# Hybrid conv/attention decoder layer on one core: the first norm's x blocks in halves, the last norm's third product on GpSimd

## The reference

```python
def reference(x, attn_norm_g, w_in, conv_w, ..., final_norm_g):
    h = rmsnorm(x, attn_norm_g)                    # x is 512 x 1024
    proj = h @ w_in                                # u_b, u_c, u_x, q, k, v, g_conv, g_attn
    y_conv = (u_b * short_conv(u_c * u_x, conv_w)) @ w_conv_out
    attn = sliding_window_attention(q, k, v, attn_sinks, rel_bias)
    mixed = sigmoid(g_conv) * y_conv + sigmoid(g_attn) * (attn @ w_attn_out)
    x = x + mixed @ w_o
    h2 = rmsnorm(x, mlp_norm_g)
    x = x + square(relu(h2 @ w_up)) @ w_down
    return rmsnorm(x, final_norm_g)

def rmsnorm(x, g):
    return x * rsqrt(mean(x * x, axis=-1) + 1e-6) * g
```

## Time and profile before

| what | us |
|---|---|
| median of 3 runs | 748.97 |
| lowest, highest | 748.92, 749.09 |
| the profiled execution's own time | 749.23 |
| its span in the profile | 747.5 |
| PE busy | 740.1 (99% of the span) |
| DVE busy | 658.7 (88%) |
| ACT busy | 429.3 (57%) |
| POOL busy | 86.0 (12%) |

### The profile page before, as it was taken

The page is one execution under the profiler, slowest core; times in us unless marked ns, Lnnn a source line. Parts: engine busy times, 40 slices in busy tenths (PEclk is TensorE's granted clock), DMA queues, the critical chain, the costliest instruction groups (busy, mean ns, idle before and its releaser), DMA issues.

```text
span 747.5 us, 10674 instructions
## 1 busy us (share of the span) xinstructions
PE 740.1 (99%) x4194; PEld 649.9 (87%) x4194; DVE 658.7 (88%) x766; ACT 429.3 (57%) x555; POOL 86.0 (12%) x119
## 2 busy tenths in 40 slices
PE   8999999999999999999999999999999999999997
PEld 8898888888888888888888899889988999899985
DVE  6997788989899687989999999998699879986998
ACT  6773555553644557564658776654465455545556
POOL 1610000111122101010100101010101010100102
PEclk9999999999999999999999999999999999999999
DMA  9898223161247987778767847777677768676703
GB/s 325 240 299 275 76 65 105 57 168 58 84 133 238 307 226 200 191 225 200 250 169 178 215 121 214 175 196 198 170 188 199 179 171 216 173 202 181 208 1 114
DMA packets 68948, 134.41 MB, mean 180 GB/s; under 512 B 2653, under 2 KB 18085, under 8 KB 68901
## 3 DMA queue, kind: packets, MB, share of 16 engines
q1 hardware_dynamic: 48880, 85.23, 33.9%
q0 software_dynamic: 19808, 48.25, 30.0%
q10 hardware_dynamic: 212, 0.28, 0.1%
HBM read 127.43 MB, written 6.32 MB: 179 GB/s over the span
## 4 chain that ended last, share of the span: by engine, by line
PE 98%; DMA 1%; ACT 0%; DVE 0%; SPq 0%; issue 0%; ACTq 0%
PE pair L1094 46%; PE pair L1049 22%; PE pair L790 6%; PE pair L792 6%; PE pair L791 6%; PE pair L916 5%; PE pair L837 2%; PE pair L812 1%; PE pair L811 1%; PE pair L821 1%; DMA xn<-in_x 1%; PE pair L851 1%; PE pair L943 0%; PE pair L945 0%; PE pair L944 0%; PE pair L1000 0%
## 5 line engine op out<-in xcount | busy, mean ns | idle before, releaser
L1406 ACT ACTIVATE high<-home_raw 128x2048 fp32r<-128x2048 f32 x91 | 174.3, 1916 | 148.1 <-PE pair L1094 102.4
L2058 DVE TENSOR_TENSOR home_lo<-home_raw,high 128x2048 fp32r<-128x2048 f32 x91 | 208.5, 2291 | 34.4 <-ACT high L1406 34.1
L1094 PE MATMUL pair<-high,s_hi_tile 128*128 128x512 f32 x440 | 110.4, 391 | 0.0
L1094 PE MATMUL pair<-high,s_lo_tile 128*128 128x512 f32 x440 | 109.9, 390 | 0.0
L1094 PE MATMUL pair<-home_lo,s_hi_tile 128*128 128x512 f32 x440 | 109.7, 390 | 0.0
L1094 PEld LDWEIGHTS pair<-home_lo,s_hi_tile 128*128 128x128 f32 x440 | 82.4, 188 | 17.5 <-DVE home_lo L2058 0.4
L1094 PEld LDWEIGHTS pair<-high,s_lo_tile 128*128 128x128 f32 x440 | 82.4, 188 | 17.1
L1094 PEld LDWEIGHTS pair<-high,s_hi_tile 128*128 128x128 f32 x440 | 81.7, 188 | 17.4 <-ACT pair L1501 0.5
L790 PE MATMUL pair<-h,wgt 128*128 128x512 f32 x192 | 76.7, 399 | 0.0
L792 PE MATMUL pair<-h,wgt 128*128 128x512 f32 x192 | 75.0, 391 | 0.0
L791 PE MATMUL pair<-h,wgt 128*128 128x512 f32 x192 | 74.9, 390 | 0.0
(11 more groups left out here) (236 smaller groups left out, 1130.1 us busy)
## 6 DMA issues: line engine op xcount, KB each, us to landing
home_raw<-in_w_up SPq DMA_DIRECT2D x16, 1024.0 KB, 5.3
home_raw<-in_w_down SPq DMA_DIRECT2D x16, 1024.0 KB, 5.1
raw<-in_w_in SPq DMA_DIRECT2D x26, 512.0 KB, 4.9
home_raw<-in_w_up POOLq DMA_DIRECT2D x12, 1024.0 KB, 8.3
home_raw<-in_w_down POOLq DMA_DIRECT2D x12, 1024.0 KB, 8.5
home_raw<-in_w_in POOLq DMA_DIRECT2D x7, 1024.0 KB, 8.6
home_raw<-in_w_in SPq DMA_DIRECT2D x7, 1024.0 KB, 6.2
home_raw<-in_w_conv_out SPq DMA_DIRECT2D x4, 1024.0 KB, 5.2
```

The lines of the kernel that those rows point to most:

```text
L1094: last = mm(pair[region(s, i)][:, b, :], a_[:, k, b * P:(b + 1) * P], w[:, k, :], start=(fresh and kind == 0 and k == 0), stop=(kind == 2 ...
L1406: a(high[n % 2][:, :], home_raw[home_of(s, name)][:, :], ACT.Copy).then_inc(m_hi, 1)
L2058: v.tensor_tensor(home_lo[home][:, :], home_raw[home][:, :], f32(high[n % 2][:, :]), ALU.subtract).then_inc(m_lo, 1)
```

## The change

Seven edits at the start and four at the end:

- x0 and x1 are each loaded as two transfers of 512 columns (x_in for the first half, x_rest for the second). DVE's share of squares waits for the second half, ACT's squares of block 0 for the first half alone, of block 1 for both.
- Block 0 is scaled in two halves, and DVE's order becomes: share of block 0, first half of block 0, share of block 1, second half of block 0, both halves of block 1.
- PE transposes all of block 0 before block 1.
- The low parts of M1's q weights are made in three pieces (rows 0 and 1, row 2, row 3) in place of two, and PE's third pass of M1 waits for each.
- `scale_x(3)` is split around the last `tile_low`, its first half one tile sooner.
- The late transposes wait tile by tile, and block 3's first four come ahead of block 2's last two.
- POOL waits for 6 low pieces in place of 5 before N4's addition (the same point in the order).
- The gain of block 3's early half moves from DVE to POOL, behind those of blocks 0 and 1.
- The root factor of block 1's early half moves from ACT to DVE, behind `scale_late(1)`.
- `scale_late(3)` and its store are cut into two pieces of 256 columns.
- The stores keep their order and are one more.

```diff
-XN_PARTS = ((0, D), (0, D // 2, D), (0, D), (0, D // 2, D))
+XN_PARTS = ((0, D // 2, D), (0, D // 2, D), (0, D), (0, D // 2, D))
...
+        LOW_ROWS = {M1: ((0, 1), (2,), (3,)), N2: ((0, 1), (2, 3))}
...
             def load_x(b):
-                sp.dma_start(xn[:, b, :], x[b * P:(b + 1) * P, :]).then_inc(x_in[b], 16)
+                if b > 1:
+                    sp.dma_start(xn[:, b, :], x[b * P:(b + 1) * P, :]).then_inc(x_in[b], 16)
+                    return
+                for c, done in ((slice(0, D // 2), x_in), (slice(D // 2, D), x_rest)):
+                    sp.dma_start(xn[:, b, c], x[b * P:(b + 1) * P, c]).then_inc(done[b], 16)
...
-            for b, late in ((0, 1), (0, 0), (1, 1), (1, 0), (2, 1), (2, 0), (3, 1)):
...
+            for b in range(TB):
+                for e in range(512 // late_size(b)):
+                    sp.wait_ge(out_late, b + e + 1)
+                    store(b, 512 * (1 - early(b)) + late_size(b) * e, late_size(b))
+                if b < TB - 1:
                     sp.wait_ge(out_early[b], 1)
-                    store(sp, b, early(b))
+                    store(b, 512 * early(b), 512)
...
-            pool.wait_ge(q_low, 5)
+            pool.wait_ge(q_low, 6)
...
             gain(0)
             gain(1)
+            gain(3)
...
-            for b, n in ((0, 1), (1, 0), (0, 2), (1, 1), (0, 3), (1, 2), (1, 3)):
+            for b, n in ((0, 1), (0, 2), (0, 3), (1, 0), (1, 1), (1, 2), (1, 3)):
                 x_pair(b, n)
...
-                        order = [(k, f) for e in range(2) for f in range(4) for k in (2 * e, 2 * e + 1)]
+                        order = [(k, f) for rows in LOW_ROWS[i] for f in range(4) for k in rows]
...
-                            elif k % 2 == 0:
-                                pe.wait_ge(q_low, 2 * at_ + k // 2 + 1)
+                            elif any(k == rows[0] for rows in LOW_ROWS[i]):
+                                pe.wait_ge(q_low, 3 * at_ + [rows[0] for rows in LOW_ROWS[i]].index(k) + 1)
...
             def late_transposes():
-                pe.wait_ge(h_ready, 8)
-                x_transposes(2)
-                x_transposes(3)
+                for b, n in ((2, 0), (2, 1), (2, 2), (3, 0), (3, 1), (2, 3), (3, 2), (3, 3)):
+                    if b == 2:
+                        pe.wait_ge(h_ready, 2 * n + 2)
+                    x_pair(b, n)
...
                 n = SQUARED[b]
+                if b == 1:
+                    act.wait_ge(x_rest[b], 16)
...
             def scale_early(b):
-                if b < 2:
-                    act.wait_ge(gained, b + 1)
-                else:
-                    act.wait_ge(gained_late, 1)
+                act.wait_ge(gained, 3 if b == 3 else b + 1)
...
             root_of(2)
-            scale_early(1)
             root_of(3)
...
-                dve.wait_ge(x_in[b], 16)
+                dve.wait_ge(x_rest[b] if b < 2 else x_in[b], 16)
...
             share_of_squares(0)
+            scale_x(0, (0,))
             share_of_squares(1)
-            scale_x(0)
-            scale_x(1)
+            scale_x(0, (1,))
+            scale_x(1, (0, 1))
...
-            q_low_half(M1, 0)
-            q_low_half(M1, 1)
-            scale_x(2)
+            for e in range(3):
+                q_low_rows(M1, e)
+            scale_x(2, (0,))
             share_of_squares(3)
-            for k in range(4, 8):
+            for k in range(4, 7):
                 tile_low(0, k)
-            scale_x(3)
-            q_low_half(N2, 0)
-            q_low_half(N2, 1)
+            scale_x(3, (0,))
+            tile_low(0, 7)
+            scale_x(3, (1,))
+            for e in range(2):
+                q_low_rows(N2, e)
...
-            def gain(b):
...
+            def scale_early_1():
+
+                dve.wait_ge(gained, 2)
+                r = res[:, 1, 512 * early(1):512 * early(1) + 512]
+                v.tensor_scalar(r, r, rms3[:, 2, 1:2], None, ALU.mult).then_inc(out_early[1], 1)
...
-                v.scalar_tensor_tensor(out=r, in0=src, scalar=rms3[:, 2, b:b + 1], in1=gfin[:, 512 * ch:512 * ch + 512],
-                                       op0=ALU.mult, op1=ALU.mult).then_inc(out_late, 1)
+                acc, n = pair[region(STAGES - 1, N4)][:, 1, :], late_size(b)
+                for c0 in range(0, 512, n):
+                    r = res[:, b, 512 * ch + c0:512 * ch + c0 + n]
+                    v.scalar_tensor_tensor(out=r, in0=acc[:, c0:c0 + n] if b == 3 else r, scalar=rms3[:, 2, b:b + 1],
+                                           in1=gfin[:, 512 * ch + c0:512 * ch + c0 + n], op0=ALU.mult, op1=ALU.mult
+                                           ).then_inc(out_late, 1)
...
             factor(1)
-            gain(3)
             scale_late(1)
+            scale_early_1()
             factor(2)
```

More of the change, by code:

```diff
@@ L354, in build @@
         x_in = [sem(f"x_in{b}") for b in range(TB)]
+        x_rest = [sem(f"x_rest{b}") for b in range(2)]
         raw_in = [sem(f"raw_in{i}") for i in range(4)]
@@ L403, in build @@
         ss3_ready, fin_step = sem("ss3_ready"), sem("fin_step")
-        gained, gained_late = sem("gained"), sem("gained_late")
+        gained = sem("gained")
         out_early, out_late = [sem(f"out_early{b}") for b in range(TB)], sem("out_late")
@@ L515, in early, with late_size @@
             return 0 if b < 2 else 1
+        def late_size(b):
+            return 256 if b == TB - 1 else 512
         block = ctx.enter_context(nc.Block())
@@ L645, in _, with store @@
             sp.dma_start(gfin[:, :], bass.AP(final_norm_g.tensor, 0, [[0, P], [1, D]])).then_inc(gfin_in, 16)
-            def store(eng, b, ch):
-                eng.dma_start(out[rows_of(b), 512 * ch:512 * ch + 512],
-                              res[:, b, 512 * ch:512 * ch + 512]).then_inc(out_done, 16)
-            for b, late in ((0, 1), (0, 0), (1, 1), (1, 0), (2, 1), (2, 0), (3, 1)):
-                if late:
-                    sp.wait_ge(out_late, b + 1)
-                    store(sp, b, 1 - early(b))
-                else:
+            def store(b, c0, n):
+                sp.dma_start(out[rows_of(b), c0:c0 + n], res[:, b, c0:c0 + n]).then_inc(out_done, 16)
+            for b in range(TB):
[3 more added lines that the diff above has]
+                if b < TB - 1:
                     sp.wait_ge(out_early[b], 1)
-                    store(sp, b, early(b))
-            sp.wait_ge(out_done, 16 * 2 * TB)
+                    store(b, 512 * early(b), 512)
+            sp.wait_ge(out_done, 16 * (2 * TB + 1))
         @block.gpsimd
@@ L854, in x_pair @@
                     last.then_inc(xt_ready, 1)
-            def x_transposes(b):
-                for n in range(4):
-                    x_pair(b, n)
             def idle_transposes(n):
@@ L896, in q_product @@
                         elif kind == 2:
-                            pe.wait_ge(q_low, at_ + 3)
+                            pe.wait_ge(q_low, at_ + 4)
                         if i in HS:
@@ L1783, in share_of_squares, with scale_x, q_low_rows @@
                                        ).then_inc(share_done, 1)
[L1785 to L1797, removed]
+            def scale_x(b, parts):
+                if 0 in parts:
+                    dve.wait_ge(root_done, b + 1)
+                    v.reciprocal(rms[:, 1, b:b + 1], rms[:, 0, b:b + 1]).then_inc(rms_step, 1)
+                    dve.wait_ge(rms_step, b + 1)
+                for e in parts:
+                    c = slice(*XN_PARTS[b][e:e + 2])
+                    v.tensor_scalar(xn[:, b, c], xn[:, b, c], rms[:, 1, b:b + 1], None, ALU.mult).then_inc(xn_ready, 1)
+            def q_low_rows(i, e):
+                at_, rows = Q_ORDER.index(i), LOW_ROWS[i][e]
+                c = cols(512 * rows[0], 512 * len(rows))
+                dve.wait_ge(q_high, 4 * at_ + rows[-1] + 1)
                 v.tensor_tensor(q_lo[i][:, c], q_raw[i][:, c], f32(q_hi[at_ % 2][:, c]), ALU.subtract).then_inc(q_low, 1)
```

6 lines of the change are left out of this document (removed).

## The result

| us | before | changed |
|---|---|---|
| median of 6 runs | 749.06 | 752.72 |
| lowest, highest | 748.92, 749.25 | 751.94, 753.01 |
| profiled execution: own time, span | 749.23, 747.5 | 751.94, 750.2 |

The changed kernel is slower: a ratio of 1.0046, interval [1.0036, 1.0056], where 748.25 was forecast and 748.85 was the upper end. Its profiled execution is the fastest of its six, so the trace shows 2.7 us of a difference of 3.66.

A forecast was written before the change was run, and what follows sets the result against it. PE's own work bounds the middle, a backlog of stores the end. Profiled 749.23 - 0.3 (start) - 0.45 (end) = 748.48, or 748.22 beside the median 748.97, given as 748.25; range 747.7 to 748.85.

The forecast's parts named there:

- POOL's third product "is free": End: block 3's gain on POOL takes 2.65 us and has some 5 us of slack before it is wanted.
- "isn't slowed beside it": End: DVE's 2048-column subtraction keeps its time beside POOL, on rows of 2.28 with POOL busy and 2.29 without.
- Rival (d): End: POOL's product lengthens the subtraction at 735.85, delaying PE; 750.55 if they take turns, slower from 0.72 growth; chance 0.04.
- "All else shifts as a block": Middle: only PE's first real work and what follows its last matmul can change the time.
- "I take nothing": Start: no cost for later issue of q rows, x2 and x3 (0.86 us), since the 16 DMA engines are full.
- Rival (e): Start: the whole load is late past 0.86 + 0.3 and the end's gain is spent: 749.0 to 749.3; chance 0.04.
- the second rival: Start: named for the case that the four x pieces come later than the two, by the skill's 1 MiB rule.
- (a): Start: the x halves come late and eat the 0.3: 748.5; chance 0.2.
- The start's -0.3: Start: with block 0 scaled and transposed first, the first matmul comes at about 9.0 in place of 9.31.
- The end's -0.45: End: two stores issued 0.4 to 0.45 sooner fill the bandwidth dip and shrink the store backlog; bounds 0 to -0.8.
- rival (b): End: the tail gives nothing, as nine stores with two short ones need what the dip gave: 748.65; chance 0.12.
- The signs named beforehand: Wrong if block 1's squares start after 6.3, subtraction over 2.35, PE waits between 9 and 740, or stores full to 746.5.

The follow-up runs named there:

- e8: Kernel before with all the end's edits, POOL's gains held by waits until the subtractions are done: 749.51 against 749.19, ratio 1.0003.
- e4: Kernel before with one edit, block 3's gain moved from DVE to POOL: 750.11 against 749.32, ratio 1.0009.
- e9: Kernel before with one more ACT wait at the start, on a load long landed: 750.47 against 749.23, ratio 1.0017.
- e14: Kernel before with the start's edits, but block 0 alone split and no further ACT wait: 751.0 against 749.26, ratio 1.0032.
- e13: Kernel before with x0 and x1 loaded by four transfers of 64 tokens by 1024 columns (4 KB rows): 753.49 against 749.26, ratio 1.005.
- e5: Kernel before with the start's new order but x0 and x1 loaded whole: 749.67 against 749.19, ratio 1.0005.
- e16: Kernel before with two more ACT waits at the start, on a load long landed: 750.49 against 749.22, ratio 1.0015.
- e10: Kernel before with gain(3) behind scale_late(1) on DVE, two lines swapped: 748.95 against 749.23, ratio 0.9995.
- e3: Kernel before with only the end's edits: 750.13 against 749.32, ratio 1.0012.
- e15: Kernel before with gain(3) behind scale_late(1) on DVE, and the last scaling and its store cut in two: 749.06 against 749.26, ratio 1.0.
- e2: Kernel before with only the start's edits: 751.75 against 749.32, ratio 1.003.
- e12: Kernel before with the start's edits, POOL's first two gains held until M3's subtraction is done: 751.21 against 749.23, ratio 1.0026.
- e6: Kernel before with only the loads of x0 and x1 cut in four, old order kept: 752.56 against 749.19, ratio 1.0046.
- e7: Kernel before with POOL's first product also waiting for block 1's early squares: 749.22 against 749.19, ratio 1.0.
- e17: Changed kernel with one further ACT wait at the start, behind the one it adds: 752.74 against 749.22 of the kernel before, ratio 1.0046.

## Why the prediction was wrong, point by point

**POOL's third product "is free", and DVE "isn't slowed beside it": wrong.** I compared 2.28 beside POOL with 2.29 without it and took the equality as proof. The equality was real, but it was a case where POOL waited: two products in 5.29 that take 2.59 alone (e8). Rival (d) named the place, the slack of 0.05 and the price per 0.1, and even that the two might take turns; its chance of 0.04 was far too low and its size (another 2.29) too high. The growth is 1.10, because what the subtraction waits for is one product of POOL, 1.3 alone (e8), and not its own length again. The Trainium skill, GPSIMD Engine Reference, Specifications, states that POOL and DVE contend for shared SBUF interfaces when the DVE instruction has two SBUF inputs. The runs bear it out, 2.29 to 3.39 (e4). I set the page aside for a row that couldn't test it.

**The first meeting wasn't in the forecast at all.** I had the middle as untouched and so "All else shifts as a block". e9 shows that it doesn't: one dead wait on ACT at the start costs 1.24 at the end, since POOL's lead over a subtraction falls from 0.56 to 0.41.

**"I take nothing" for four transfers: wrong in size and in its ground.** The ground was that the engines are full (share 1.03), so that transfers wait for engines and not for SP. With more transfers they weren't full: 0.83 and 0.86. I put block 1 0.1 late, 0.4 if short rows cost, 0.86 if the cover failed; the profiled execution has 0.57, and the others with four half-row pieces 1.08 to 1.82. That spread may be what the median of the changed kernel has beyond its trace, 3.66 against 2.7, but only one of its executions was traced. Rival (e) had the mechanism, at 749.0 to 749.3; the size was again too small. The Trainium skill, DMA: Bandwidth & Descriptors, Rules for kernel authors, wants transfers of 1 MiB or more for full bandwidth; e14 and e13 agree with its direction. (The prediction gave that page to "the second rival"; late loads are rivals (a) and (e).)

**The start's -0.3: not there.** Without the split loads (e5) the first q matmul comes 0.06 sooner. The step that failed is "block 0's eight transposes and the parameter tile are through by about 7.9, block 1's eight run 8.03 to 8.98": with block 0 there, the first pair and the parameter tile alone took PE from 6.80 to 7.50, where three at 0.12 would be 0.36, and then fourteen followed without a gap, 7.50 to 9.25 on PE. DVE's first gain waited for one of them (8.71 where 8.47 was forecast) and the first q matmul waited for DVE's gains. What PE lacked was neither block. e16 says the same: with block 1 read 0.43 sooner, q came at 33.83, within the spread of 33.68 to 33.90.

**The end's -0.45: half there, and given back.** DVE freed early does fill the dip, but the time from ACT's last squares to the end of the span falls by 0.2 to 0.25 (5.33 to 5.13 in e10, 5.08 in e3), not 0.45. In the changed kernel it is 5.42. There the scaling of block 0's late half starts 0.62 behind its reciprocal (741.24 to 741.86), where e10 and e15 have 0.27. Runs with the start's new order but not the end's edits show the same 0.62 and a tail of 5.61 to 5.65 (e2, e5, e12, e14), so the new order comes with 0.3 at the tail and the end's edits give 0.2 back. Why isn't known: e13, in the old order, has it too (0.62, 5.64), and e6 has not (0.27, 5.26). With e5's subtractions and q unchanged, this 0.3 is what its 0.48 has to show in the trace. Of rival (b) one part holds: the short pieces give nothing (e15 beside e10).

**The signs named beforehand** told it rightly: block 1's squares after 6.3 (6.55), a subtraction beside the third product over 2.35 (3.40), PE waiting between 9 and 740 (1.03 for M3's low part).

**The sum.** Medians: the start's edits cost 2.43 (e2), the third product 0.79 (e4), together 3.22 of 3.66. Inside the start the first meeting is worth up to 1.24 (e9) and the rest is the late load and the 0.3 at the tail; e12, with the gains held, still costs 1.98, of which holding POOL takes some (PE waits 0.47 there and 0.38 in e8). How the remaining 0.4 divides isn't settled, since block 1's landing differs by over 1 us from run to run.

## What to carry to other kernels

Before you call an engine's row "unharmed beside another", ask whether the other was working: compare its time with the same operation alone, and if it is double, your row shows one engine waiting, and the next placement may turn the roles. Where two engines that slow each other start within half a microsecond, an edit far away can decide who goes first, so look for a subtraction with no slack behind it before adding a product beside it. A semaphore keeps such a product clear of it, but check what else it then meets: in e8 and e12 that was the next subtraction. Splitting a load to start sooner delays the one behind it; price the second transfer, not the first, by a run.

## What the runs showed of the hardware that I had not expected

- A 2048-column subtraction of DVE with two SBUF inputs takes 2.28 or 3.38 beside POOL's 512-column product, nothing between. In the long case POOL's product always ends about 1.24 behind the subtraction's start. M3's took 3.38 or 3.39 when POOL started 0.41 or 0.42 ahead (eight kernels), N4's 3.38 to 3.40 when the third product started 0.16 to 0.72 ahead (four). M3's took 2.28 or 2.29 when POOL's first product, with another queued behind it, started 0.55 to 0.57 ahead (eight kernels) or 0.24 behind (e7). Who wins isn't a matter of who starts first by these rows, and the rule stays open.
- One instruction more on ACT at the start, 720 us earlier, left its rows alone up to 720 us and then put one high part 0.28 late (2.57 idle to 2.85; e9, e16, e17). On DVE the like is seen at the scaling of block 0's late half: 0.62 behind its reciprocal instead of 0.27 in every kernel with the start's new order and in e13. Both are steps of about 0.3 for which the trace names no releaser but the old one.
- The clock of TensorE fell to its lower level for some 3 us after PE had waited 2.02 us (e6), and behind a wait of 3.47 us in e13, where it stood at 0.50 from 10 to 14 us and the long run of q matmuls began at 38.48.
